# First block's layer norms: squares of x taken two columns at once, pairs added by GpSimd, four products of sums in place of eight

## The reference, cut to what matters

```python
def layer_norm(x, g, b):
    xf = x.astype(jnp.float32)
    mu = jnp.mean(xf, -1, keepdims=True)
    var = jnp.mean(jnp.square(xf - mu), -1, keepdims=True)
    return ((xf - mu) * lax.rsqrt(var + LN_EPS) * g + b).astype(x.dtype)

for l in range(DEPTH):                      # DEPTH = 2
    mix = even_mixer(...) if l % 2 == 0 else odd_mixer(...)
    x = layer_norm(ALPHA * x + mix, ln1_g[l], ln1_b[l])
    hdn = jnp.square(jax.nn.relu(x @ ffn_w1[l]))
    x = layer_norm(ALPHA * x + hdn @ ffn_w2[l], ln2_g[l], ln2_b[l])
    e = rms_norm(p[l] @ ple_w_proj[l], ple_norm_g[l])
    x = x + jax.nn.sigmoid(x @ ple_w_gate[l]) * e
```

## Time and profile before

| what | value |
|---|---|
| median of 3 runs | 1821.57 us (1821.32 to 1824.0) |
| the profiled execution, its own time | 1823.08 us |
| its span in the trace | 1821.8 us |
| PE busy | 1767.1 us, 97% |
| DVE busy | 1293.4 us, 71% |
| ACT busy | 1003.5 us, 55% |
| POOL busy | 78.3 us, 4% |
| granted TensorE clock, mean | 0.993 |

### The profile page before, as it was taken

The page is one execution under the profiler, slowest core; times in us unless marked ns, Lnnn a source line. Parts: engine busy times, 40 slices in busy tenths (PEclk is TensorE's granted clock), DMA queues, the critical chain, the costliest instruction groups (busy, mean ns, idle before and its releaser), DMA issues.

```text
span 1821.8 us, 35759 instructions
## 1 busy us (share of the span) xinstructions
PE 1767.1 (97%) x14744; PEld 1651.1 (91%) x14744; DVE 1293.4 (71%) x2428; ACT 1003.5 (55%) x1795; POOL 78.3 (4%) x81
## 2 busy tenths in 40 slices
PE   7999999999999999999999999999999999999997
PEld 6787999978888999999999998899999998689997
DVE  6656656668888755876776777776765887776666
ACT  5655545466656544655764655454654665554544
POOL 0000200020001100000200010100100000100000
PEclk9999999999999999999999999999999999999999
DMA  9978866686434556455455453446565553245663
GB/s 372 372 286 296 294 192 185 186 290 202 128 116 134 172 176 196 129 160 176 150 188 162 150 164 115 130 153 193 188 188 186 170 154 108 77 139 185 185 185 116
DMA packets 93715, 334.68 MB, mean 184 GB/s; under 512 B 10976, under 2 KB 12832, under 8 KB 93424
## 3 DMA queue, kind: packets, MB, share of 16 engines
q1 hardware_dynamic: 91872, 327.27, 55.5%
q0 software_dynamic: 1680, 5.11, 0.9%
HBM read 331.29 MB, written 1.05 MB: 182 GB/s over the span
## 4 chain that ended last, share of the span: by engine, by line
PE 91%; DVE 5%; ACT 2%; DMA 1%; issue 1%; ACTq 0%; DVEq 0%
PE bank L617 25%; PE bank L619 24%; PE bank L618 24%; PE bank L657 2%; PE bank L988 2%; PE bank L938 2%; PE bank L658 2%; PE bank L659 2%; PE bank L803 2%; PE bank L963 2%; PE bank L1295 1%; DVE low L591 1%; DVE low_side L591 1%; DMA pT<-in_p 1%; PE bank L1928 0%
## 5 line engine op out<-in xcount | busy, mean ns | idle before, releaser
L591 DVE TENSOR_TENSOR low<-ring,high 128x1024 fp32r<-128x1024 f32 x410 | 500.9, 1225 | 180.3 <-ACT high L583 173.0
L583 ACT CAST high<-ring 128x1024 fp32r<-128x1024 f32 x410 | 429.0, 1046 | 229.3 <-PE bank L619 205.2
L617 PE MATMUL bank<-XHx,high 128*128 128x256 f32 x1720 | 499.1, 290 | 17.8 <-DVE low L591 9.1
L618 PE MATMUL bank<-XLx,high 128*128 128x256 f32 x1720 | 485.3, 282 | 0.0
L619 PE MATMUL bank<-XHx,low 128*128 128x256 f32 x1720 | 484.9, 282 | 0.0
L617 PEld LDWEIGHTS bank<-XHx,high 128*128 128x128 f32 x1720 | 326.2, 190 | 33.8 <-DVE low L591 9.1
L618 PEld LDWEIGHTS bank<-XLx,high 128*128 128x128 f32 x1720 | 326.5, 190 | 1.0 <-issue 0.2
L619 PEld LDWEIGHTS bank<-XHx,low 128*128 128x128 f32 x1720 | 326.4, 190 | 0.0
L617 PE MATMUL bank<-XHc,high_side 128*128 128x256 f32 x608 | 178.3, 293 | 9.4 <-DVE low_side L591 8.4
L618 PE MATMUL bank<-XLc,high_side 128*128 128x256 f32 x608 | 172.6, 284 | 0.0
L619 PE MATMUL bank<-XHc,low_side 128*128 128x256 f32 x608 | 172.5, 284 | 0.0
(11 more groups left out here) (469 smaller groups left out, 3572.9 us busy)
## 6 DMA issues: line engine op xcount, KB each, us to landing
ring<-in_stream SPq DMA_DIRECT2D x410, 512.0 KB, 3.7
ring_side<-in_stream SPq DMA_DIRECT2D x110, 512.0 KB, 3.7
ring_mod<-in_stream SPq DMA_DIRECT2D x96, 512.0 KB, 7.6
x_nb<-in_rpb POOLq DMA_DIRECT2D x6, 256.0 KB, 3.8
x_late_NB<-in_rpb POOLq DMA_DIRECT2D x6, 256.0 KB, 3.1
Xx<-in_x SPq DMA_DIRECT2D x2, 512.0 KB, 5.7
Xc<-in_ctx SPq DMA_DIRECT2D x1, 1024.0 KB, 7.1
out<-y SPq DMA_DIRECT2D x8, 128.0 KB, 2.0
```

What stands on the lines that cost most here:

```text
L583: nc.scalar.copy(st.high[:, j % st.n_split, :], st.ring[:, j % st.n_ring, :]).then_inc(*A.tick(st.s_high, A_us(TB * P), (st.name, "high", j)))
L591: nc.vector.tensor_tensor(st.low[:, j % st.n_ring, :], st.ring[:, j % st.n_ring, :], st.high[:, j % st.n_split, :].bitcast(F32), ALU.subtr ...
L617: nc.tensor.matmul(out, wh, xh, start=(i == 0), stop=False)
L618: nc.tensor.matmul(out, wh, xl, start=False, stop=False)
```

## The change

Three parts. ScalarE squares two columns in one instruction of 512 elements (four in place of eight, in each norm), into both halves of a slot. GpSimd adds the two halves in place (four new instructions of 256 elements in each norm). TensorE sums four products in place of eight. The second block's norms, of x and of the context, are left as they are.

```diff
@@ tensor_layer_norm
-    yield from tensor_squares(k, w, tag)
+    b = yield from w.banks.take(T, (tag, "log"))
+    k.bank_of[tag, "squares"] = b
+    for i in range(DC // 2):
+        T.wait_ge(k.s_pool, (yield tag, "paired", i))
+        T.shape(P, P)
+        nc.tensor.matmul(k.bank[b][:, 0:SEQ], k.c["meanD"][:, :], w.SQ[:, k.sq_of[tag, i], 0:SEQ], start=(i == 0),
+                         stop=(i == DC // 2 - 1)).then_inc(*T.tick(k.s_sums, T_us(SEQ, 4), (tag, "summed", i)))
+        yield None
@@ scalar_layer_norm
-    for i in range(DC):
-        A.wait_ge(k.s_x_done, (yield tag, "centred", i // 2))
+    for i in range(DC // 2):
+        A.wait_ge(k.s_x_done, (yield tag, "centred", i))
         j = k.sq_of[tag, i] = yield from w.sq.take(A, (tag, "summed", i))
-        nc.scalar.activation(w.SQ[:, j, 0:SEQ], w.X[:, i, :], ACT.Square).then_inc(
-            *A.tick(k.s_squares, A_us(SEQ), (tag, "square", i)))
-    A.wait_ge(k.s_sums, (yield tag, "summed", DC - 1))
+        nc.scalar.activation(w.SQ[:, j, :].rearrange("p (a t) -> p a t", t=SEQ), w.X[:, 2 * i:2 * i + 2, :],
+                             ACT.Square).then_inc(*A.tick(k.s_squares, A_us(2 * SEQ), (tag, "squares", i)))
+    A.wait_ge(k.s_sums, (yield tag, "summed", DC // 2 - 1))
@@ gpsimd_layer_norm
+    for i in range(DC // 2):
+        G.wait_ge(k.s_squares, (yield tag, "squares", i))
+        sq = w.SQ[:, k.sq_of[tag, i], :]
+        nc.gpsimd.tensor_tensor(sq[:, 0:SEQ], sq[:, 0:SEQ], sq[:, SEQ:2 * SEQ], ALU.add).then_inc(
+            *G.tick(k.s_pool, 0.75, (tag, "paired", i)))
     for i in range(DC):
         x = w.X[:, i, :]
```

## The result

The changed kernel takes 1826.43 us in the median of 20 runs (1822.86 to 1829.73), the kernel before 1822.81 us in 20 runs beside them (1819.00 to 1826.97). The ratio is 1.0019, with a 95% interval of 1.0012 to 1.0026. So it is 3.6 us slower. I had said 1820.4 us, 1.2 us faster; the time lies inside my range, on the other side of no change. Three runs stand outside all comparisons, of 9717 and 1968 us of the kernel before and of 8758 us of plan_vector, whose only trace is of that run.

A forecast was written before the change was run, and what follows sets the result against it. PE, busy for 97% of the span, was taken as the bound, with norm 1 bound by its chain. Terms -1.2 - 1.1 + 2.8 - 1.7 = -1.2 us took the 1821.6 us median to 1820.4 us, range 1815 to 1828.

The forecast's parts named there:

- Norm 1, 1.2 us gained: Norm 1, bound by its chain: Ln starts 1.2 us earlier, all gained; 0.5 us with adds of 1.03 us.
- Norm 2, 1.1 gained: Norm 2: sums lose 1.7 us, Ln at 383.9 against 384.26; 1.1 us gained, bounds 1.7 gained and 0.5 lost.
- Norm 3, 2.8 lost: Norm 3: moved orders stall PE behind the mean; 2.8 us lost, bounds 1.7 gained and 4.6 lost.
- The first product of x at about + 14.7, as before: Norm 3: x's first product about 14.7 us after the mean, against 14.8 before.
- I take nothing for it: Odd mixer and parts of the second block: the planner's new order counted as 0, with 3 us either way.
- new ones come for old ones: Stretches the planner reorders, such as the odd mixer: PE's waits are short, and new waits replace old ones.
- Norm 4, 1.7 gained: Norm 4: context products cover the adds, four sums come off PE; 1.7 us gained, bounds 3.4 gained and 1 lost.
- The sum: Whole kernel: the four norms' terms total -1.2 us, giving a median of 1820.4 us.
- a late GpSimd: Rival, norm 1: GpSimd starts its first add late, 1828.9 us at worst; 20%, counting pair adds of 1.03 us or more.
- about 175.6: Norm 1: a first GpSimd add starting after about 175.6 us outlasts p and decides the chain.
- about 181: Norm 1: the kernel is slower by over 0.2% only if the first GpSimd add starts after about 181 us.
- all of PE's saved work arrives: Rival, whole kernel: norm 3's hole is refilled, gain near 16 times 0.43 us, 1814.7; 25%, with other ways below 1818.

The follow-up runs named there:

- plan_vector: Kernel before, nothing edited, only the planner's cost of a VectorE instruction 1% higher, giving another order from the odd mixer on: 1834.49 us, ratio 1.0073.
- edit_only: The edit in all four norms, every other instruction in the order of the kernel before: 1824.81 us against 1822.88, ratio 1.0011 (0.9999 to 1.0022).
- norm2_kept_fill: The edit in norm 2 alone, in the order of the kernel before, with no fill despite the label: 1820.71 us against 1822.36, ratio 0.9996.
- order_only: The changed kernel's order on all engines with the work of the kernel before in it: 1827.15 us against 1822.88, ratio 1.0021.
- fill_after: The changed kernel with useless TensorE products added at ten stalls: 1827.82 us, ratio 1.0030 to the kernel before.
- norms_1_2: The edit in norms 1 and 2 only, planned anew, against the kernel before: 1827.41 us, ratio 1.0026.
- norms_3_4: The edit in norms 3 and 4 only, planned anew, against the kernel before: 1825.94 us, ratio 1.0017.
- plan_scalar: Kernel before, nothing edited, only the planner's cost of a ScalarE instruction 1% higher, changing the order from the start: 1832.00 us, ratio 1.0055.
- the first four experiments: edit_only, order_only, norms_1_2 and norms_3_4, against the kernel before: ratios 1.0011, 1.0021, 1.0026 and 1.0017.

## Why the prediction was wrong, step by step

**Norm 1, 1.2 us gained.** Ln comes 1.1 us sooner behind centring, the stage gains 0.8. Right within 0.4 us, and for the reason given: p is what the chain waits for, and the add takes 0.71 us where I took 0.70.

**Norm 2, 1.1 gained.** 2.3 were. The edit itself gives 1.1 (edit_only and norm2_kept_fill, 1.1 each; after against order_only 1.0), the new order the rest. Ln starts 1.2 us sooner than before once the lead with which this stage begins (1.9 us) is taken off; I had counted 0.4, and PE's wait behind it is 1.32 us for the 2.4 that I had.

**Norm 3, 2.8 lost.** The mechanism was right in kind and place, a stall of 3.95 us behind the mean (I had 3.65) and a table load in front of Ln. The size was not. From product 1007 to 1132 the changed kernel loses 5.9 us, 5.2 without the two context products that it does more there. Two sub-steps failed. "The first product of x at about + 14.7, as before": it came at + 17.0. I had the last two squares done at + 7.5; the fourth pair's square began only at + 8.2, since its slot came free with the second sum, which stood behind the context's recurrence and ran at half clock. And the sum had no term for the clock: 10.2 us at half clock go with the stall. In fill_after, with the stall filled and none of it, this part is 1.3 us shorter; PE's idle time in it, 5.0 us for 1.7 before, is the larger piece. That the new order itself brings the loss, and not the adds, is shown by order_only and norms_1_2, which have it too (81.3 and 81.7 us for 76.7); outside of that order the edit costs 1.1 us there in edit_only and 0.4 in norms_3_4.

**The odd mixer, "I take nothing for it".** From product 779 to 1007 it is 1.2 us longer, with two context products (0.7 us) fewer done: 1.9 us. I had "new ones come for old ones", and for the longest wait that is so, 1.55 us for 1.47. But PE is idle 0.6 us longer from product 874 to 1007, and 3.4 us at half clock, which the kernel before didn't have there, cost up to 1.7 more; in fill_after, where the wait is filled, the same part is 1.4 us shorter.

**Norm 4, 1.7 gained.** 2.6 in the profile, 0.9 without the difference of 3.4 us at half clock. Nobody waits for the adds, as forecast.

**The sum.** My four terms and the odd mixer's nothing gave -1.2. Read from the stages, -0.8 - 2.3 + 1.9 + 5.2 - 0.9 is + 3.1, and the medians say + 3.6. The step that failed is thus the pair norm 3 and odd mixer, 2.8 us forecast and 7.1 measured: norm 3's late chain was priced too low, and the odd mixer and the clock behind stalls were put at nothing. One slip bore on nothing, since no add was late: by the steps given for a late GpSimd, Ln comes 4.55 us behind the first add, so the thresholds for that add are 174.8 and 179.6, not "about 175.6" and "about 181".

**What stood behind it.** I took the planner's new order as noise around nothing, 3 us either way. Five kernels with a new order (order_only, norms_1_2, norms_3_4, plan_vector, plan_scalar) were slower by 3 to 13 us, and none faster. So the old order is better than all five tried. How it stands among orders in general isn't shown: norms_1_2 shares the changed kernel's order up to product 1007, and norms_3_4 the old one. That a re-planned order is slower by itself should have been my rival on the far side, in place of the late GpSimd, which the rows refute. The rival "all of PE's saved work arrives" fell as well: even in the old order, edit_only isn't faster.

**What stays open.** Edit_only's median is 1.9 us above before with an interval that reaches no change, and its norm 1 stalls for 3.36 us partly because p came later in that execution. How the medians' 3.6 us split over stages is read from single executions, which differ by chance in where the clock falls: from product 1132 to the end the changed kernel took 1169.97 us, order_only with the same order 1172.31. No run moved one instruction of the new order back, so which of them costs norm 3 its time (the table load and the context's gate ahead of the squares, or the first sum ahead of all fillers) is argued from the rows and not shown.

## What to carry to other kernels

Where a planner lays out the whole program, an edit is two changes, its own and the new order's. Make both kernels, the edit in the old order and the old work in the new order, before believing in either; here the second alone was as slow as the whole change, and the first alone wasn't faster than the kernel before. Moving work off a busy engine gains only where its wait for the helper is covered: the four sums gained in norm 2, where the embedding filled the gaps, and lost in the old order of norms 3 and 4. And price a stall of TensorE ahead of dense work at more than its length.

## What the runs showed of the hardware

In the kernel before, 33 runs (those beside the first four experiments) span 0.990 to 0.997 in mean granted clock, and their times go with it (correlation -0.91, 1.3 us for each 0.001). At a clock of 0.992 or 0.993 its 13 runs average 1824.5 us, and after's three 1824.5 too; but before has 0.994 in the mean and after 0.990. So most of the spread of a kernel's runs is where the clock happens to fall. Equal times at an equal clock don't make the clock the cause, as the stages around norm 3 in fill_after show. By this slope, an estimate, the lower mean clock of order_only's runs (0.9920, beside 0.9942) would go with 2.9 of its 4.3 us, but that of plan_scalar's (0.9930, beside 0.9943) with 1.7 of 9.6: there the loss is waits.

In the traces the falls come in or behind stalls of PE of 1 us and more, and not behind each. The wait of 2.98 and 2.95 us at 1195 has one in before and after, and none in edit_only (2.98 us at 1200). The Trainium skill (TensorE: Matmul & The Clock Gate, What's actually happening) has it that idleness lowers the clock to half and activity restores it, at a moment that isn't tied to the kernel; the traces agree, with the clock down behind two of five nearly equal stalls, 1.72 to 1.78 us.

On GpSimd the sum of two tensors of 256 elements took 0.73 us in the median of 16 (0.71 to 1.45), the sum of a tensor and one value per partition 1.03 us (0.92 to 2.03). Where VectorE was idle during the operation it was 0.72 us for the one and 0.92 for the other, so the operation with less to read is the slower one; all in these two traces that took over 1.2 us had VectorE busy for half of the time or more.
